# The product of gelu and G moved from VectorE to GpSimd in a dense expert stage

## The reference

```python
def block(args):
    xt, et, gt = args
    act = jnp.einsum('td,tkd->tk', xt, u_tab[et])
    return jnp.einsum('tk,tkd->td', jax.nn.gelu(act, approximate=False) * gt, v_tab[et])
```

## Time and profile before

| | us |
|---|---|
| median of 3 runs | 1743.4 (1741.38 to 1743.91) |
| span of the profiled execution, first to last instruction | 1738.7 |
| PE busy | 1666.5 (96%) |
| DVE busy | 1554.8 (89%) |
| ACT busy | 866.7 (50%) |
| POOL busy | 654.3 (38%) |
| DMA rate in the dense stage | about 400 GB/s |

### The profile page before, as it was taken

The page is one execution under the profiler, slowest core; times in us unless marked ns, Lnnn a source line. Parts: engine busy times, 40 slices in busy tenths (PEclk is TensorE's granted clock), DMA queues, the critical chain, the costliest instruction groups (busy, mean ns, idle before and its releaser), DMA issues.

```text
span 1738.7 us, 29907 instructions
## 1 busy us (share of the span) xinstructions
PE 1666.5 (96%) x9344; PEld 1402.2 (81%) x9344; DVE 1554.8 (89%) x3196; ACT 866.7 (50%) x2431; POOL 654.3 (38%) x644
## 2 busy tenths in 40 slices
PE   6999999999966999999999999999999999999997
PEld 4566777866645788899989999999999988999996
DVE  3887863499999999999999999999999999999998
ACT  3222564346778995444444444444444444444443
POOL 0000000034557994444444444344444444443442
PEclk9999999999977999999999999999999999999999
DMA  9343202211135779999999999999999999999996
GB/s 357 125 141 123 74 1 78 71 61 49 61 121 173 223 201 346 396 389 401 408 395 401 405 407 401 403 409 395 396 407 399 396 406 400 402 402 403 400 400 211
DMA packets 129316, 505.91 MB, mean 291 GB/s; under 512 B 9184, under 2 KB 64096, under 8 KB 79968
## 3 DMA queue, kind: packets, MB, share of 16 engines
q0 software_dynamic: 36864, 268.45, 38.3%
q1 hardware_dynamic: 92096, 236.49, 36.5%
q10 hardware_dynamic: 288, 0.13, 0.0%
HBM read 477.18 MB, written 25.10 MB: 289 GB/s over the span
## 4 chain that ended last, share of the span: by engine, by line
DVE 35%; DMA 23%; PE 19%; issue 19%; ACT 2%; POOL 2%; DVEq 1%; SPq 0%; POOLq 0%; ACTq 0%
DMA slab<-table,ixr 22%; DVE slab L1745 9%; PE psum L501 7%; DVE slab L1695 5%; DVE ulo L1636 4%; PE psum L736 3%; DVE slab L1735 3%; DVE slab L1699 2%; DVE vlo L1722 2%; DVE slab L1730 2%; PE psum L502 2%; PE psum L666 1%; DVE wlo L1718 1%; POOL slab L1876 1%; DVE slab L1550 1%
## 5 line engine op out<-in xcount | busy, mean ns | idle before, releaser
L1876 POOL DMA_INDIRECT slab<-table,ixr x256 | 421.5, 1647 | 603.8 <-DVE slab L1745 552.2
L848 PE MATMUL psum<-hhi,uhi 128*128 128x384 f32 x1008 | 338.8, 336 | 2.4 <-issue 2.1
L848 PE MATMUL psum<-hhi,ulo 128*128 128x384 f32 x1008 | 338.2, 335 | 0.0
L848 PE MATMUL psum<-hlo,uhi 128*128 128x384 f32 x1008 | 337.6, 335 | 0.0
L1745 DVE SCALAR_TENSOR_TENSOR slab<-slab,cf 128x1024 f32<-128x1024 f32 x252 | 323.3, 1283 | 14.8 <-DVE slab L1745 0.5
L1735 DVE SCALAR_TENSOR_TENSOR slab<-slab,h2tok 128x1024 f32<-128x1024 f32 x256 | 312.2, 1220 | 26.5 <-DMA slab<-table,ixr 26.2
L862 PE MATMUL psum<-vhi,whi 128*128 128x512 f32 x762 | 297.1, 390 | 3.1 <-DVE wlo L1718 3.1
L862 PE MATMUL psum<-vhi,wlo 128*128 128x512 f32 x762 | 299.7, 393 | 0.0
L862 PE MATMUL psum<-vlo,whi 128*128 128x512 f32 x762 | 299.2, 393 | 0.0
L501 PE MATMUL psum<-slab 128*128 128x512 f32 x464 | 239.1, 597 | 2.1 <-ACT slab L929 1.7
L1210 ACT CAST whi<-slab 128x384 fp32r<-128x384 f32 x127 | 65.3, 514 | 306.7 <-DVE slab L1730 306.7
(11 more groups left out here) (237 smaller groups left out, 2801.3 us busy)
## 6 DMA issues: line engine op xcount, KB each, us to landing
slab<-ublk SPq DMA_DIRECT2D x64, 1024.0 KB
slab<-vtab SPq DMA_DIRECT2D x63, 1024.0 KB
slab<-wblk SPq DMA_DIRECT2D x90, 512.0 KB, 4.6
g_dram<-slab SPq DMA_DIRECT2D x11, 1984.0 KB, 9.0
slab<-g_dram SPq DMA_DIRECT2D x31, 704.0 KB, 8.9
slab<-table,ixr POOLq DMA_INDIRECT x256, 9.2
slab<-slab SPq DMA_DIRECT2D x42, 64.0 KB, 10.1
x<-x_in SPq DMA_DIRECT2D x1, 2560.0 KB, 9.6
```

The costliest lines, as they stand in the source:

```text
L848: last = pe.matmul(psum[:, b, 0:ND], w[:, c, :], m[:, c, :], start=(m_ == 0), stop=(m_ == 3 * DC - 1))
L1876: pool.indirect_dma_start(out=rows[:, sl % GR, :], out_offset=None, in_=table, in_offset=bass.IndirectOffsetOnAxis(ap=ixr[:, half, half_co ...
```

## The change

For the keys 2 to 127 the product of gelu and G leaves DVE's program and goes to GpSimd's, behind the two gathers of the next key. On DVE the subtraction that makes `wlo` stood between the two dots and now stands behind both. Nothing else changes; the product waits for the same two semaphores and increments the same one.

```diff
@@ -1790,10 +1790,9 @@
                         v.wait_ge(ulo_set, 4)
                     if not (last and jj == JB - 1 or first and jj < 3):
                         u_rest(n + 1, (jj + 1) % JB)
-                    weigh(n, jj)
                     dot(n, jj, k, 0)
+                    dot(n, jj, k, 1)
                     w_rest(n, jj)
-                    dot(n, jj, k, 1)
                     for e in range(2):
                         add_row(n, jj, k, e, fresh=fresh and jj == 0)
 
@@ -1889,6 +1888,14 @@
                     fetch_row(sl, half, sl % 8)
 
 
+            def weigh(n, jj):
+
+                pool.wait_ge(gel_set, n + 1)
+                pool.wait_ge(g_in[jj // QUAD], 4 * n - 4 * jj + 32)
+                m = jj % QUAD
+                wb = wgt[:, jj % 4, :].rearrange("p (g t) -> p g t", t=TG)
+                pool.tensor_tensor(wb, wb, gin[:, jj // QUAD, :, m * TG:(m + 1) * TG], ALU.mult).then_inc(w_set, 1)
+
...
@@ -1915,12 +1922,17 @@
...
             for n in range(2, JB + 1):
                 fetch_pair(n, n, n // 4 + 1, True)
+                if n > 2:
+                    weigh(n - 1, n - 1)
             with pool.Fori(1, STEPS - 1) as i:
                 for jj in range(JB):
                     fetch_pair(i * JB + (jj + 1), jj + 1, i * 2 + ((jj + 1) // 4 + 1))
+                    weigh(i * JB + jj, jj)
             for jj in range(JB - 1):
                 n = KEYS - JB + jj + 1
                 fetch_pair(n, jj + 1, n // 4 + 1, True)
+                weigh(n - 1, jj)
+            weigh(KEYS - 1, JB - 1)
```

## The result

| | before | after |
|---|---|---|
| median, us | 1742.4 (1739.8 to 1743.9, 4 runs) | 1767.6 (1763.7 to 1772.4, 4 runs) |
| ratio | 1 | 1.0149, 95% interval 1.0128 to 1.0169 |
| span of the profiled execution, us | 1738.7 | 1770.6 |
| vlo of key 3 to vlo of key 126, us a key | 8.3315 | 8.5576 |

The change makes the kernel slower by 1.5%, 25 us. The forecast was 1768. The profiled execution (1772.4) lies 4.7 us above the median of its kernel, so its rows carry a little more than the median: of the 31.9 us by which its span is longer, the 123 keys give 27.8 (123 x 0.2261), the start up to key 3 gives 2.1 and the end 2.0.

A forecast was written before the change was run, and what follows sets the result against it. TensorE's 8.306 us a key bounds, DVE close behind at 8.09. DVE becomes 7.63 + 0.80 hold + 0.10 late rows = 8.53 against 8.331, over 123 keys + 24.5 us: 1768 us, range 1738 to 1800 (0.83).

The forecast's parts named there:

- What bounds it: Dense stage: TensorE's 8.306 us a key is the floor, DVE's 8.09 hides behind it; anything above is paid once a key.
- The hold, 0.80 us: DVE's second dot: GpSimd's product keeps it out of SBUF for 0.80 us a key, between 0.67 and 0.99.
- the four places: Trace spots, L1915, L1742, L1583 and the copy at 1112.28, where GpSimd and DVE keep each other out; losses 2.13 and 1.07 us.
- The product's 0.99 us: GpSimd's product of 384 columns takes 992 ns, from 457 for 128 columns and 2.09 ns a further column.
- The time of asking, T + 3.17: T is a key's vlo start; GpSimd's product asks at T + 3.17, 0.25 us before the first dot ends.
- Rival 2: GpSimd asks too late for the gap after the first dot, DVE idles before wlo: + 107, 1850 us; chance 0.14.
- ACT's cover: ACT's cast and coefficient after the product: cf ready near T + 5.7, wanted at T + 5.84, cover 0.15 us.
- The order costs nothing: DVE's wlo behind both dots: finds whi ready with 0.35 us to spare, and TensorE wants wlo far later.
- the fifth step of the prediction: Gathered rows: GpSimd holds the second dot back anyway, so a row may come until 12.65 instead of 12.44 us.
- Late rows, 0.10 us a key: Second dot waiting for gathered rows: 0.62 us in one key of four, taken as 0.10 a key, between 0 and 0.20.
- Rival 1: DVE isn't held, or only in time it waits anyway; TensorE's 8.306 decides: 1740 us; chance 0.18.
- rival 3: DVE loses the whole 0.99 us and rows are as late as before: 8.72 to 8.82 a key, 1791 to 1803 us; chance 0.12.

The follow-up runs named there:

- Experiment 3: Kernel before plus a spare GpSimd product of 128x384, which nobody waits for, behind each pair of gathers: 1854.4 us, ratio 1.0650.
- experiment 4: Kernel before plus a GpSimd memset of 128x384 into a spare tile behind each pair of gathers: 1741.6 us, ratio 0.9995.
- experiment 8: Kernel after, with GpSimd multiplying only 192 of the 384 columns (dense result wrong): 1755.8 us, ratio 1.0071.
- experiment 5: Kernel after, with a GpSimd memset of 128x384 into a spare tile ahead of each product: 1790.2 us, ratio 1.0268.
- experiment 6: Kernel after, with GpSimd's product also waiting for the first dot of its key: 1850.4 us, ratio 1.0618.
- experiment 1: Kernel before with only wlo moved behind both dots, DVE keeping the product: 1755.9 us, ratio 1.0075.
- experiment 11: Kernel after, with the loop's gathers bringing 4 KB a token instead of 8 (gathered result wrong): 1761.2 us, ratio 1.0105.
- experiments 9 and 10: G's loop load cut to one group behind the first: in the kernel after 1773.1 us; in the kernel with only wlo moved 1748.1 us, ratio 1.0037.
- experiments 3 and 7: Spare GpSimd product in the kernel before: without a wait 1854.4 us; waiting for DVE's own product of the key 1791.9 us, ratio 1.0283.

## Why the prediction was right, point by point

**What bounds it: right.** DVE's 8.09 lay 0.22 under TensorE's 8.306, and what went above was paid once a key. The wait before L848 that was predicted for every key is there, 102 times, mostly 0.07 us behind ulo's end, but the profile names it "issue", and with 0.43 us on average (44.0 / 102) the weight load's gap is twice the 0.2 that was expected.

**The hold, 0.80 us: right, shown.** 2.03 - 1.22 = 0.81, and the period 8.43 to the hundredth. Experiment 3 shows that shared access is the cause and not the data, experiment 4 that a writing instruction doesn't do it, experiment 8 that it goes with the columns. The loss read from the four places in the search and the first keys carried over to another shape.

**The product's 0.99 us: right.** It is shown with 1.01 to 1.20, 1.18 in most keys and 1.93 in one. In the key above 0.23 of the 1.18 pass before the first dot gives way at 1121.71, which leaves 0.95.

**The time of asking, T + 3.17: wrong, without harm.** I took the shown start as the request and left it 0.25 us before the gap. GpSimd asks at T + 2.3 to T + 2.7 in experiment 3, whose gathers stand in the same place, so here the margin is 0.7 us or more. A request 0.4 us later changed the size of the hold (experiment 5), not who goes first. Rival 2's mechanism and price were right (experiment 6: 9.18 and 1850.4 against 9.20 and 1850), its point of decision was not, and the 0.14 that it got was too much.

**ACT's cover: right, larger than told.** The 0.15 us that I allowed behind GpSimd did not show: whi starts at T + 4.39 instead of T + 4.5, and the coefficient has 0.43 us to spare instead of 0.15.

**The order costs nothing: wrong as a step, right in the sum.** I costed wlo's move only by what waits for wlo. But it also brings the second dot forward by 0.47 us, which alone costs 12 us (experiment 1). In the whole change this doesn't show up, since GpSimd holds the dot until about T + 4.2, which is what the fifth step of the prediction said.

**Late rows, 0.10 us a key: about right in size, by another way.** In the profiled execution the mean key is 8.558, 0.128 above 8.43. Two pauses of GpSimd, which I had not priced, are 0.029 of it (1.87 + 1.74 over 123), and the rest, 0.098, goes to late rows; experiment 11 gives 0.09, and by medians 0.05. The way there was not as told. I had one key in four wait, for 0.83 us, with 0.21 of it covered. Measured are 45.3 / 59 = 0.77 us in every second key, 0.39 us a key. That is over the 0.3 which the prediction itself named as the sign of a mis-sized DMA term. It costs so little because a wait now begins at T + 3.42 and its first 0.81 us fall into time in which GpSimd would hold the dot anyway: of the 45.8 us that the timeline shows, the parts beyond 0.81 add up to 9.7, 0.08 a key. That more keys wait and that the cover is larger came out even, which is partly luck. Why more rows are late is only in part settled: shorter rows end it (experiment 11), G's load decides in which keys it falls and not how much there is in sum (experiments 9 and 10), and whose transfers delay a row when G's don't stays open.

**The sum.** Forecast + 24.5 us, measured + 25.2 between medians and + 31.9 between profiled executions, of which the start and the end, costed at nothing, gave 4.1. That the forecast and the medians agree within 1 us is luck: the executions of the kernel after differ by 8.7 us among themselves, and the pauses, the start and the end stood at nothing. One reading of the prediction was wrong without harm to the difference. It took the 4.7 us between the span of 1738.7 and the median of 1743.4 for what lies around the span. In the kernel after that is 1.8 us in every execution (1772.4 against 1770.6), so the other 2.9 say that the profiled execution of the kernel before was one of the shorter ones, an estimate from those two numbers. This, with the 4.7 by which the kernel after's was long, is why the profiles lie 31.9 us apart and the medians 25.2. Rival 1 (no hold) fell with the 2.03 us, rival 3 (the whole 0.99 charged) with the 0.81.

## What to carry to other kernels

Before an elementwise product goes from DVE to GpSimd, price what DVE's next two-input instruction loses to it, not only what it frees: here 0.46 us left DVE and 0.81 came back. A write-only instruction on GpSimd was free beside the same work. And moving an instruction is two edits, one for who waits for it and one for each instruction that it lets forward: if that one needs a transfer in a stage with full DMA engines, the transfer must have the slack. And when DMA is full, look at which keys wait before and after a transfer is cut, and not at the total alone: the wait can move.

## What the runs showed of the hardware

- A GpSimd instruction behind an indirect DMA can hold DVE before its own start is shown, by 0.46 us at least (experiments 3 and 7).
- With the DMA engines at a share of 0.97 and more (1000 to 1100 us), the load of G, 0.7 MB every fourth key, decides in which key a gathered row is late; without it other rows are late (experiments 9 and 10).
- GpSimd pauses in the dense stage before a second gather, twice in the kernels before and after. Here is the first in the timeline of POOL in the kernel after, followed by DVE's:

```profile
1126.25 1.45 POOL L1875 DMA_INDIRECT slab<-table,ixr  x1 [2.46 <-DVE slab L1745]
1130.33 1.97 POOL L1875 DMA_INDIRECT slab<-table,ixr  x1 [2.63 <-issue]
```

And DVE, same view and columns:

```profile
1133.91 0.56 DVE L1718 TENSOR_TENSOR wlo<-slab,whi 128x384 fp32r<-128x384 f32 x1 [2.43 <-ACT whi L1210]
```

The usual gap there is 0.30 us. The kernel before has such pauses too, of 2.67 us near 1120 and of 2.69 near 1578, and the keys in which they lie take 8.1 us as elsewhere; with the product behind the gathers it makes a key of 10.3 us, and the second, near 1602, one of 10.2. Its cause is not in the profile. Work that DVE waits for inherits the irregularities of the queue it is put on.
